# Two conditioning groups moved to the end of layer 0's experts, with squares summed a stage ahead

## The chip, the cores and the metric

One core of a Trainium2 chip runs the whole program. The metric is device time in microseconds (us). The kernel is one launch: one batch of 512 latent tokens with 256 context tokens and their conditioning vectors goes in, the latents after two blocks of two layers each come out, all in float32. The weights are read from HBM once.

## The reference, cut to what matters

Four layers follow each other. The first block's two layers are the ones that the change touches:

```python
for l in range(DEPTH):                        # DEPTH = 2, D = 1024
    mod_l = (silu_c @ w_ada[l] + b_ada[l])[:, None, :]      # w_ada [2, 1024, 6144]
    mod_c = (silu_cc @ w_ada[l] + b_ada[l])[None, None, :]
    sh1, sc1, g1, sh2, sc2, g2 = jnp.split(mod_l, 6, axis=-1)   # and the same of mod_c
    h_l = modulate(x_lat, norm_mix[l], sh1, sc1)            # rmsnorm(x, g) * (1 + sc) + sh
    h_c = modulate(x_ctx, norm_mix[l], sh1c, sc1c)
    # layer 0: mixer_ab (low-rank attention and grouped-query attention, rotary)
    # layer 1: mixer_na (attention to a window of neighbours and to the context)
    x_lat = x_lat + g1 * o_l
    h_l = modulate(x_lat, norm_ffn[l], sh2, sc2)
    if not last:                                            # layer 0: context too, 768 tokens
        x_ctx = x_ctx + g1c * o_c
        h_c = modulate(x_ctx, norm_ffn[l], sh2c, sc2c)
        y = hier_moe(tokens, w_rg[l], b_rg[l], w_re[l], b_re[l], w_gate[l], w_up[l], w_down[l])
        x_ctx, x_lat = x_ctx + g2c * y_c, x_lat + g2 * y_l
    else:                                                   # layer 1: the 512 latents
        x_lat = x_lat + g2 * hier_moe(h_l, ...)
return rmsnorm(x_lat, norm_final)

def hier_moe(h, ...):
    pg = softmax(h @ w_rg + b_rg); g_sel = argmax(pg)       # one of 4 groups
    le_sel = (h @ w_re + b_re)[group g_sel]                 # its 8 experts
    top_p, top_i = top_k(softmax(le_sel), 2)
    gate_w = p_gsel * top_p / sum(top_p)
    # each token goes to its two experts of 32:
    # y = sum gate_w * ((silu(x @ w_gate[e]) * (x @ w_up[e])) @ w_down[e])
```

A second block of two layers with other mixers (retention and sparse attention, an mLSTM) and dense feed-forward parts follows. The change does not touch it, apart from the first norm in it, which is the `norm_final` above.

## The kernel before, in words

**Layout.** Activations are feature-major: `P.x` (the residual) and `P.h` are tiles of 128 partitions x 8 chunks x 768 tokens, 256 of context first. The program is a sequence of stages, each a block with one program per engine, and they meet only in semaphores. `P.ahead` and `Ahead` objects hold the loads that a stage starts for the next one.

**Conditioning** (`class Conditioning`, lines 402 to 479). `w_ada` of both layers is 48 units of 1 MB, in six groups of eight (three groups a layer: shift and scale of the mixer; its gate and the shift of the experts; their scale and gate). `multiply` makes four matmuls of a unit (L448), which add up in one PSUM bank over the eight units of a group. `copy` (ScalarE, L455) takes the bank, `turn` (TensorE, L462) transposes it with four matmuls, `bias` (VectorE, L470 to L478) adds `b_ada` and makes the scales. A `Beside` object ties units and groups to the steps of a stage: after product n of the stage, PE multiplies the units listed for n, and the group listed for n is turned. Units 0 to 15 go with the first norm and the first projection, 16 and 17 with the norms of the low-rank parts, 18 to 36 with the low-rank up-projections (stage `ab_up`, `product_stage`, products at L1176), and 37 to 47 with the rotary stage (`rope_stage`), behind which the distance table's product stands (L2990).

**Norm** (`norm_stage`, line 555; `LatNorm`, line 679). Squares of eight chunks on ScalarE (L599, L604) and VectorE, their sums with matmuls against ones (L636, or L540 inside `QuadRows`), a root on ScalarE, a reciprocal on VectorE, a spread of the rows over the partitions on PE, then per chunk a scaling on VectorE and a shift on ScalarE (L617). `slab` gives POOL the split of the first weight slab of the next projection into two float32r parts (`FirstSlab.pool`, L243 and L245).

**Output stages** (`out_stage`, line 1686, on `split_stage`, line 877). Products of split float32r weights in eight PSUM banks (L996); VectorE takes each with `add_scaled` (L1227), which adds gate times product to `P.x`. ScalarE is free after the splits.

**Experts** (`expert_stage`, line 1843). The order of the work is laid down by `ExpertPlan`: 32 experts, two of them fixed first, the others in the order of their load, which is known only at run time. An expert is six pieces of 1 MB: gate and up in halves (4), down in halves (2). A ring of 18 slots holds them: 12 tiles of its own, three in `P.h`, two in `P.ahead`, one called `late`. SP issues the loads (L1800) in the plan's order; piece n behind the first 18 waits until the piece before it in its slot is freed (`used`). Twelve pieces and the route's inputs (L1830 to L1838) are issued in the norm stage. In order, the opening of the stage is:

1. PE: router logits of all tokens (L2221, 36 columns of weights against `P.h`), ScalarE and VectorE copy them, PE turns them (L2228). VectorE works out each token's experts, their counts, ranks (L2245, L2246) and slots.
2. PE turns `P.h` into rows of tokens (L2237), ScalarE copies them (L2347) and issues their store to a DRAM table (L2349).
3. PE finds the tokens of the two fixed experts with one-hot matmuls (L2252), VectorE makes their numbers, POOL gathers these rows from the DRAM table (L1879).
4. PE turns the gathered rows into features (`turn_rows`, L1936), makes the slot table for all experts (L2264), and starts the first visit.

A visit (`wide`, L1957, L1972, L1973; `down`, L1965, L1979, L1980) is 64 or fewer token slots of one expert; layer 0 has 41 of them, layer 1 has 36. ScalarE makes the silu (L1984), VectorE the product (L1987), ScalarE copies the result (L2387), POOL stores it to a table in DRAM (L2173, L2177) and gathers the rows of later visits. The first release of a ring slot comes with the first visit's first half.

The end of the stage is the mix: POOL gathers each token's two results (L2212), ScalarE scales one by its weight (L2421), VectorE adds the other (L2586), PE turns the tile back (L2338), VectorE adds it times the gate to `P.x` (L2598, eight instructions a tile). Layer 0 has six tiles of 128 tokens, layer 1 four.

On SP, the opening has these waits in the order of the pieces (L2121 to L2130):

```python
if n == plan.OWN - 1:  sp.wait_ge(turned_ready, NT)                  # P.h is free
if n == plan.OWN + 2:  [sp.wait_ge(rows_out[m], 16) for m in range(IN_AHEAD)]   # P.ahead is free
if n == plan.RING - 1: sp.wait_ge(first_slots, 1)                    # `late` is free
if n >= plan.RING:     sp.wait_ge(used, plan.freed[plan.after[n]])
```

**Order of the stages**, with the microseconds of the trace at which each runs: load and first norm 0 to 56, ab_in to 183, low-rank norms to 199, ab_up to 286, rotary to 319, attention to 541, ab_out 545 to 615, norm to 634, layer 0's experts to 1220, norm (`mod1`) to 1239, na_in to 1437, attention and na_out to 1609, norm to 1624, layer 1's experts to 2181, then the second block.

## Time and profile before

| | |
|---|---|
| median of 3 runs | 3599.15 us |
| lowest, highest | 3592.58, 3599.3 us |
| the profiled execution | 3606.98 us, span 3605.1 us |
| mean granted clock of TensorE | 0.928 |
| PE busy | 3134.4 us (87%) |
| PE's weight loads | 2150.2 us (60%) |
| VectorE, ScalarE, POOL busy | 1453.9 (40%), 761.6 (21%), 269.1 us (7%) |
| DMA | 675.08 MB, mean 187 GB/s |

Times of the rows below count from the start of the span. "Busy" of a matmul group is from its first start to its last end; PE is TensorE's matmuls, PEld its weight loads, which run beside them. PEclk is the granted clock as a share of the full 2.4 GHz, so 0.50 is 1.2 GHz. In the timelines each line is a group of like instructions on one engine: start, busy time, engine, line of the source, operation, out<-in, shape, count, and in brackets the idle time ahead of the group and what ended it. In the page's part of 40 slices a slice is 90 us.

### The profile page before, as it was taken

The page shows a single profiled execution, that of the slowest core. Times are in us where ns is not written, and L with a number is a line of the kernel's source. Part 1 is how long each engine was busy: PE and PEld are TensorE (multiplying, and loading weights), DVE is VectorE, ACT ScalarE, POOL GpSimd, SP SyncE. Part 2 cuts the span into 40 slices and gives each one's busy share as a digit, 9 for nine tenths or more (in the row PEclk, how much of TensorE's full clock was granted, in tenths as well). Part 3 has the DMA queues.
Part 4 walks back from the last instruction along what each step waited for, and adds up shares of the span by engine and source line. Part 5 has one row for each costly group of instructions (what it writes and reads, how often), then busy time and mean ns, then how long its engine had stood idle before and what let it go on. Part 6 is the DMA issues. An engine that isn't in the chain of part 4 may idle for free. (4 is left out here: it accounts for less than half of the span.)

```text
span 3605.1 us, 48930 instructions
## 1 busy us (share of the span) xinstructions
PE 3134.4 (87%) x19227; PEld 2150.2 (60%) x19227; DVE 1453.9 (40%) x2502; ACT 761.6 (21%) x1477; POOL 269.1 (7%) x471
## 2 busy tenths in 40 slices
PE   6999998798887599786987567988999999899998
PEld 5734677333333498663333336866888778678886
DVE  4225564300000533663000006455565574555555
ACT  3013571211111301631111111142110111221101
POOL 0000040111111200001111111000000000000000
PEclk8999999799998699897999878999999998999998
DMA  7176822999999424619999984212333175023321
GB/s 251 55 294 178 204 21 61 363 389 391 403 398 412 142 72 67 74 52 385 393 405 406 407 348 144 78 42 79 96 93 112 41 101 75 24 82 102 105 91 53
DMA packets 349969, 675.08 MB, mean 187 GB/s; under 512 B 68275, under 2 KB 275220, under 8 KB 294359
## 3 DMA queue, kind: packets, MB, share of 16 engines
q1 hardware_dynamic: 334396, 635.41, 52.8%
q0 software_dynamic: 13312, 31.49, 2.6%
q10 hardware_dynamic: 2067, 5.48, 0.4%
q8 instruction: 135, 2.21, 0.3%
q14 instruction: 59, 0.48, 0.0%
HBM read 639.00 MB, written 45.09 MB: 190 GB/s over the span
## 5 line engine op out<-in xcount | busy, mean ns | idle before, releaser
L3735 ACT ACTIVATE ffn_mixed<-ffn_mixed 128x512 f32<-128x512 f32 x44 | 27.8, 632 | 394.1 <-DVE ffn_mixed L3656 394.1
L1972 PE MATMUL moe0b_wide_ps<-moe_raw,moe0b_feats 128*64 128x512 f32 x208 | 98.2, 623 | 14.5 <-DMA moe_raw<-in_moe_w_up 14.5
L1987 DVE TENSOR_TENSOR moe0b_hidden<-moe0b_hidden,moe0b_wide_ps 64x512 f32<-64x512 f32 (+1 forms) x21 | 12.7, 603 | 239.1 <-ACT moe0b_hidden L1984 239.1
L1987 DVE TENSOR_TENSOR moe1b_hidden<-moe1b_hidden,moe1b_wide_ps 64x512 f32<-64x512 f32 (+1 forms) x18 | 10.3, 573 | 234.7 <-ACT moe1b_hidden L1984 234.7
L1987 DVE TENSOR_TENSOR moe0b_second<-moe0b_second,moe0b_wide_ps 64x512 f32<-64x512 f32 (+1 forms) x20 | 12.2, 611 | 227.6 <-ACT moe0b_second L1984 227.6
L1987 DVE TENSOR_TENSOR moe1b_second<-moe1b_second,moe1b_wide_ps 64x512 f32<-64x512 f32 (+1 forms) x18 | 10.3, 573 | 220.8 <-ACT moe1b_second L1984 220.8
L1973 PE MATMUL moe0b_wide_ps<-moe_raw,moe0b_feats 128*64 128x512 f32 x208 | 98.5, 624 | 0.0
L3653 DVE TENSOR_SCALAR ffn_mixed<-ffn_gate_ps,all_cols 128x512 f32<-128x512 f32 x44 | 35.6, 810 | 145.7 <-PE ffn_up_ps L3585 141.1
L1496 DVE TENSOR_REDUCE attn_top<-attn_scores 128x1 f32<-128x768 f32 (+1 forms) x96 | 72.4, 776 | 38.0 <-PE attn_scores L1409 38.0
L243 POOL CAST second_first_hi<-all_ahead 128x1024 fp32r<-128x1024 f32 x8 | 9.7, 1218 | 997.0 <-DMA all_ahead<-in_ffn_w_up 711.2
L1465 ACT ACTIVATE attn_probs_t<-attn_turned 128x512 f32<-128x512 f32 x112 | 63.4, 604 | 82.4 <-PE attn_turned L1423 82.4
L1972 PE MATMUL moe1b_wide_ps<-moe_raw,moe1b_second 128*64 128x512 f32 x120 | 63.0, 676 | 19.3 <-DMA moe_raw<-in_moe_w_up 19.2
L1979 PE MATMUL moe0b_result_ps<-moe_raw,moe0b_outputs 128*64 128x512 f32 x160 | 73.3, 598 | 4.2 <-DMA moe_raw<-in_moe_w_down 4.2
L1980 PE MATMUL moe0b_result_ps<-moe_raw,moe0b_outputs 128*64 128x512 f32 x160 | 73.4, 598 | 0.0
L1879 POOL DMA_INDIRECT moe_rows_in<-h_rows,moe_slot_token x73 | 69.7, 954 | 37.8 <-issue 21.7
L1456 ACT ACTIVATE l_cq<-attn_scores,attn_top 128x768 f32<-128x768 f32 (+1 forms) x96 | 71.7, 756 | 0.7 <-DVE attn_top L1496 0.7
L3656 DVE SCALAR_TENSOR_TENSOR ffn_mixed<-ffn_gate_ps,all_cols,ffn_mixed 128x511 f32<-128x511 f32 x88 | 65.9, 749 | 12.0 <-DVE ffn_mixed L3653 0.3
L1972 PEld LDWEIGHTS moe0b_wide_ps<-moe_raw,moe0b_feats 128*64 128x64 f32 x208 | 28.1, 143 | 71.2 <-issue 70.6
L3585 PE MATMUL ffn_gate_ps<-ffn_x_hi,ffn_w_hi 128*128 128x512 f32 x176 | 68.5, 389 | 0.0
L3585 PE MATMUL ffn_gate_ps<-ffn_x_lo,ffn_w_hi 128*128 128x512 f32 x176 | 68.5, 389 | 0.0
L3585 PE MATMUL ffn_gate_ps<-ffn_x_hi,ffn_w_lo 128*128 128x512 f32 x176 | 68.5, 389 | 0.0
L3585 PE MATMUL ffn_up_ps<-ffn_x_hi,ffn_w_hi 128*128 128x512 f32 x176 | 68.5, 389 | 0.0
(998 smaller groups left out, 8829.3 us busy)
## 6 DMA issues: line engine op xcount, KB each, us to landing
moe_raw<-in_moe_w_gate SPq DMA_DIRECT2D x88, 1024.0 KB, 28.5
moe_raw<-in_moe_w_up SPq DMA_DIRECT2D x88, 1024.0 KB, 28.9
moe_raw<-in_moe_w_down SPq DMA_DIRECT2D x86, 1024.0 KB, 29.1
all_ahead<-in_ffn_w_up SPq DMA_DIRECT2D x88, 512.0 KB, 5.1
all_h<-in_moe_w_gate SPq DMA_DIRECT2D x26, 1024.0 KB, 28.3
all_h<-in_w_ada SPq DMA_DIRECT2D x23, 1024.0 KB, 6.6
all_h<-in_moe_w_down SPq DMA_DIRECT2D x21, 1024.0 KB, 30.4
ffn_down<-in_ffn_w_down SPq DMA_DIRECT2D x40, 512.0 KB, 3.6
```

The lines of the kernel that those rows point to most:

```text
L1456: nc.scalar.activation(raised[k % LEAD][s][:, 0:t.keys], src[:, 0:t.keys], ACT.Exp, bias=column(top, k, s), scale=-1.0 if biased else 1.0, ...
L1465: nc.scalar.activation(probs_t[k % 2][:, at:end, :], turned[n % RING][:, 0:end - at, :], ACT.Copy).then_inc(turned_taken, 1)
L1496: V.tensor_reduce(column(top, k, s), scores[k % LEAD][s][:, 0:t.keys], AX.X, ALU.max, negate=True).then_inc(topped, 1)
L1879: nc.gpsimd.indirect_dma_start(rows, None, P.h_dram[0:n_tok, :], bass.IndirectOffsetOnAxis(ap=tokens, axis=0), bounds_check=n_tok - 1, oob ...
L1972: nc.tensor.matmul(wide_ps[n][LOW, :], x[:, c, :], gate[:, at], start=c == 0, stop=c == DC - 1)
L1973: last = nc.tensor.matmul(wide_ps[n][HIGH, :], x[:, c, :], up[:, at], start=c == 0, stop=c == DC - 1)
L1979: nc.tensor.matmul(result_ps[n][LOW, :], columns[n][:, c, :], rows[:, at:at + BANK], start=c == 0, stop=c == EC - 1)
L1980: last = nc.tensor.matmul(result_ps[n][HIGH, :], columns[n][:, c, :], rows[:, at + BANK:at + D], start=c == 0, stop=c == EC - 1)
L1987: return nc.vector.tensor_tensor(hidden[n][HIGH, 0:cols], hidden[n][HIGH, 0:cols], wide_ps[n][HIGH, 0:cols], ALU.mult)
L3585: last = nc.tensor.matmul(out[s][:], lhs_t, rhs, start=k == 0, stop=k == 3 * DC - 1)
L3653: V.tensor_scalar(mixed[s][:], gate_ps[s][:], col(taps + (FFN_CONV - 1) * FC), col(shift), ALU.mult, ALU.add).then_inc(conv_step, 1)
L3656: V.scalar_tensor_tensor(mixed[s][:, back:], gate_ps[s][:, 0:SEQ - back], col(taps + (FFN_CONV - 1 - back) * FC), mixed[s][:, back:], ALU. ...
```

## The change

It has five parts.

A. Units 32 to 47 of the conditioning, groups 4 and 5 (layer 1's mixer gate and all but the first shift and scale), move to the end of `expert_stage` of layer 0. Eleven are loaded into ring slots as the last visits free them, five behind the loop for experts with too many tokens. PE multiplies eight and turns group 4 ahead of the mix, and multiplies two behind each of the first four tiles' turns; group 5 is turned behind the last tile's turn. The copies and biases stand on ScalarE and VectorE ahead of the mix and at its end.

```diff
+LATE_GROUP = 4
-            ada.place("later", spare, range(2 * DC, ada.GROUPS * DC))
+            ada.place("later", spare, range(2 * DC, LATE_GROUP * DC))
...
                 product_stage(nc, P, "ab_up", loads, products, banks=5, ahead=tables,
-                              beside=Beside(ada, range(21, 42), {2 * n: (18 + n,) for n in range(19)}, {12: (2,), 28: (3,)}))
+                              beside=Beside(ada, range(21, 29), {5 * n: (18 + n,) for n in range(6)}, {28: (2,)}))
...
             rope_stage(nc, P, "rope", tables, items, spread,
-                       Beside(ada, range(42, 48), {n + 3: (37 + n,) for n in range(11)}, {6: (4,), 13: (5,)}), distances)
+                       Beside(ada, range(29, 32), {n + 3: (24 + n,) for n in range(8)}, {11: (3,)}), distances)
...
+                for u, n in zip(now, late_slots):                       # SP, behind the last expert piece
+                    sp.wait_ge(used, plan.freed[last_in[n]])
+                    ada.fetch(sp, u)
                 sp.wait_ge(used, 4 * N)
...
+                for u in then:                                          # SP, behind the extras
+                    ada.fetch(sp, u)
...
+                for u in late_units[0:DC]:                              # PE
+                    ada.multiply(pe, u)
+                if ada is not None:
+                    ada.turn(pe, LATE_GROUP)
                 for t in range(NT):
...
                     last.then_inc(mix_turned, 1)
+                    if t >= 2:
+                        tally_tile(t - 2)
+                    for u in late_units[DC + 2 * t:DC + 2 * t + 2]:
+                        ada.multiply(pe, u)
+                if len(late_units) > DC:
+                    ada.turn(pe, LATE_GROUP + 1)
+                tally_tile(NT - 2)
+                tally_tile(NT - 1)
...
+                if ada is not None:                                     # DVE
+                    ada.bias(dve, LATE_GROUP)
                 mix(0)
                 for t in range(NT):
                     if t + 1 < NT:
                         mix(t + 1)
+                    if t == NT - 1 and len(late_units) > DC:
+                        ada.bias(dve, LATE_GROUP + 1)
```

ScalarE has `ada.copy(act, LATE_GROUP)` ahead of its loop and `ada.copy(act, LATE_GROUP + 1)` behind it.

B. The two output stages ahead of the experts sum the squares of what they write and take the root. They have two, and one, PSUM banks fewer for it. The norm of the experts (`rooted=True`) then begins with the reciprocal.

```diff
+    def square(self, act, j):                                          # class Tally
+        out = self.squares[j % 2] if j else self.sums
+        self.nc.scalar.activation(out[:], self.P.x[:, j, self.all], ACT.Square).then_inc(self.squared, 1)
+    def add(self, dve, j):
+        if 0 < j < DC - 1:
+            self.nc.vector.tensor_tensor(self.sums[:], self.sums[:], self.squares[j % 2][:], ALU.add).then_inc(self.added, 1)
...
+        root, at = root_rows(self.P, self.n_tok), 0
+        for quads, total in zip(self.quads, self.total):
+            self.nc.scalar.activation(root[:, at:at + quads.m], total[:, 0:quads.m], ACT.Sqrt, scale=1.0 / D,
+                                      bias=self.P.eps[:, 0:1]).then_inc(self.rooted, 1)
```

The squares of seven chunks are added up before PE sums them against ones; the last chunk's are summed by themselves.

C. The router's logits are made in the norm stage from the rows that are not normalised yet. POOL multiplies the router's weights by the gains and by the shifts, PE multiplies with `P.x`, ScalarE copies, VectorE scales by the reciprocal root, and PE adds up the shifts' part.

```diff
+    def fold(self, pool):                                              # class EarlyLogits
+        pool.wait_ge(self.inputs.w_in, 2 * 16)
+        for w in self.which:
+            for out, by in ((self.gained, P.scale[:, self.l, 1, :, w]), (self.shifted, P.mod[:, self.l, 3 * DC:4 * DC, w])):
+                self.nc.gpsimd.tensor_tensor(out[:, w], w_route[:], by.unsqueeze(2).to_broadcast([PART, DC, self.W]), ALU.mult)
...
             for n in steps:                                             # norm_stage, PE
                 quads[n].spread(by_half[n], P.pick, root[:, cols[n]], root_spread)
+            if logits is not None:
+                for c in range(C):
+                    logits.multiply(pe, c, jobs)
+                logits.shift(pe)
```

D. The first visits' features are made with one-hot matmuls from the rows in SBUF, 48 of them in layer 0 and 32 in layer 1, instead of the gather. The slot table stands behind the first visit's wide half. The rows are stored with the columns in another order, so that `turn_rows` reads them contiguously.

```diff
+                def first_rows():
+                    pe.wait_ge(rows_act, NT)
+                    pe.wait_ge(first_made, 1)
+                    for c in range(DC):
+                        for t in range(NT):
+                            by_chunk = row_places[t].rearrange("t (c p) -> t c p", c=DC)
+                            hot = first_hot[:, t * FIXED:(t + 1) * FIXED, :].rearrange("p e n -> p (e n)")
+                            last = nc.tensor.matmul(feats_ps[:, c, :], by_chunk[:, c, :], hot, start=t == 0, stop=t == NT - 1)
+                    last.then_inc(feats_ready, 1)
...
-                pe.wait_ge(rows_act, NT)
-                rows(0)
-                slot_table()
+                first_rows()
                 for s in range(N):
+                    if s == 1:
+                        slot_table()
...
                     if n == plan.OWN + 2:                               # SP
+                        sp.wait_ge(feats_ready, 1)
                         for m in range(IN_AHEAD):
                             sp.wait_ge(rows_out[m], 16)
                     if n == plan.RING - 1:
-                        sp.wait_ge(first_slots, 1)
```

E. Both mixes square the finished tiles (ScalarE), sum them (PE, `tally_tile`, eight matmuls a tile) and take one root at the end. The norm `mod1` and the final norm begin with the reciprocal (`rooted=True`, `made=True`).

```diff
+                def square_tile(t):                                     # ScalarE
+                    act.wait_ge(mix_added, (t + 1) * DC)
+                    nc.scalar.activation(squares[t % 2], P.x[:, :, at:at + PART], ACT.Square).then_inc(mix_squared, 1)
...
+                act.wait_ge(mix_summed, NT)
+                nc.scalar.activation(root_rows(P, n_tok), result_ps[0][:, 0:n_root], ACT.Sqrt, scale=1.0 / D, bias=P.eps[:, 0:1])
```

## Rows read from the trace of the kernel before

**Rows 1.** Page, busy share of the DMA engines in 40 slices of 90 us

```profile
DMA  7176822999999424619999984212333175023321
```

**Rows 2.** DMA view of 700 to 1100

```profile
DMA packets 24908, 158.17 MB, mean 395 GB/s; under 512 B 4331, under 2 KB 4339, under 8 KB 6891
...
moe_rows_in<-h_rows,moe_slot_token POOLq DMA_INDIRECT x34, 8.4
```

**Rows 3.** Windows: stretch, length, PE, PEld, DVE, ACT, POOL, PEclk, DMA, GB/s

```profile
200.00:240.00 40.00, 40.00 (x164) 16.25 (x162) 5.17 (x9) 3.52 (x9) 0.00 (x0) 1.00 0.74 270
...
674.00:680.00 6.00, 6.00 (x30) 5.93 (x28) 0.22 (x2) 2.31 (x2) 1.71 (x4) 0.50 0.71 294
...
1200.00:1210.00 10.00, 5.91 (x26) 5.12 (x27) 8.08 (x21) 3.44 (x3) 4.15 (x5) 0.50 0.77 262
```

**Rows 4.** Timeline of ab_up and the end of the rotary stage

```profile
226.26 1.07 PE L448 MATMUL ada_acc<-all_h,all_cond 128*32 128x512 f32 x8
...
227.25 4.11 PE L1176 MATMUL ab_up_bank<-l_cq,ab_up_wq 128*96 128x512 f32 x12
...
232.32 0.65 PE L462 MATMUL ada_turned<-all_ident,ada_rows 128*128 128x128 f32 x4
...
316.80 1.24 PE L2990 MATMUL rope_distance_acc<-ab_up_wkv,rope_bias 33*8 33x512 f32 x4
```

**Rows 5.** Timeline, end of ab_out and opening of layer 0's experts

```profile
614.33 0.75 DVE L1227 SCALAR_TENSOR_TENSOR all_x<-ab_out_bank,all_mod,all_x 128x512 f32<-128x512 f32 x1 [4.98 <-PE ab_out_bank L996]
...
622.20 0.43 SPq L1800 DMA_DIRECT2D moe_raw<-in_moe_w_gate  x1
...
634.51 7.70 PE L2221 MATMUL moe0b_feats_ps<-all_h,moe_w_route 128*36 128x384 f32 x32 [9.59 <-PEq L558]
...
655.33 1.02 ACT L2347 ACTIVATE moe_rows_in<-moe0b_wide_ps 128x1024 f32<-128x1024 f32 x1 [0.68 <-PE moe0b_wide_ps L2237]
...
674.90 5.22 PE L2264 MATMUL moe0b_slot_ps<-moe0b_outputs,moe0b_second 128*128 128x64 f32 x24
```

**Rows 6.** GB/s in 40 slices, 625 to 705 and 1640 to 1706

```profile
GB/s 430 418 434 422 430 422 418 418 410 422 426 403 418 428 430 408 416 418 270 365 422 416 422 436 414 426 242 0 0 154 211 276 328 270 406 422 418 426 422 414
...
GB/s 412 427 427 432 422 427 429 415 442 422 427 425 417 412 427 422 253 25 104 161 181 415 370 283 355 437 407 422 412 432 417 412 437 412 358 315 278 387 402 447
```

**Rows 7.** Timeline of PE, the first visit of layer 0 and of layer 1

```profile
680.05 1.12 PE L1972 MATMUL moe0b_wide_ps<-moe_raw,moe0b_feats 128*64 128x512 f32 x1
...
1667.40 1.12 PE L1972 MATMUL moe1b_wide_ps<-moe_raw,moe1b_feats 128*64 128x512 f32 x1
```

**Rows 8.** Timeline, end of mod1, and start of the second block

```profile
1233.64 5.33 ACT L617 ACTIVATE all_h<-mod_squares,all_mod 128x512 f32<-128x512 f32 x8
...
1234.79 2.36 POOL L245 TENSOR_TENSOR na_v_first_lo<-all_ahead,na_v_first_hi 128x1024 fp32r<-128x1024 f32 x1
...
2193.59 0.79 PE L954 MATMUL even_in_bank<-even_in_x_hi,second_first_hi 128*128 128x512 f32 x1 [5.86 <-POOL second_first_lo L245]
```

**Rows 9.** Timeline of PE in 1636 to 1640, ranks of layer 1

```profile
1637.30 0.49 PE L2245 MATMUL moe1b_result_ps<-moe1b_second,moe_earlier 128*128 128x128 f32 x2 [1.36 <-DVE moe1b_second L2461]
...
1637.63 0.39 PE L2246 MATMUL moe1b_result_ps<-moe1b_second,all_ones 128*128 128x128 f32 x2
```

**Rows 10.** Timeline of VectorE, mix of layer 0

```profile
1196.67 1.28 DVE L2586 SCALAR_TENSOR_TENSOR moe_raw<-moe_raw,moe_weight 128x1024 f32<-128x1024 f32 x1 [21.18 <-ACT moe_raw L2421]
...
1218.26 2.16 DVE L2598 SCALAR_TENSOR_TENSOR all_x<-moe0b_wide_ps,all_mod,all_x 128x128 f32<-128x128 f32 x8
```

**Rows 11.** DMA of 1150 to 1190 in 40 slices, and of 1184 to 1221

```profile
GB/s 426 410 410 410 414 434 401 426 434 401 434 410 422 438 426 393 401 393 369 377 360 377 344 336 303 287 238 139 123 82 49 41 39 39 16 0 8 66 0 0
...
DMA packets 1779, 6.39 MB, mean 173 GB/s; under 512 B 224, under 2 KB 224, under 8 KB 1776
```

**Rows 12.** DMA view of 634 to 700, first gathers

```profile
moe_rows_in<-h_rows,moe_slot_token POOLq DMA_INDIRECT x4, 3.8
```

**Rows 13.** Timeline of PE, the norm of the second block's feed-forward

```profile
2483.18 1.95 PE L540 MATMUL ffn_norm_single<-all_x,all_ones 128*32 128x128 f32 x64 [1.05 <-PEq L883]
```

306 lines of the change are left out of this document (219 added, 87 removed).

## Prediction, made before the changed kernel ran

> **What bounds the kernel now.** On one core no single engine bounds all 3605.1 us, so I went stage by stage. The page's slices come first [rows 1]: DMA stands at 9 in slices 7 to 12 and 18 to 23, the experts of layers 0 and 1, at about 400 GB/s, and low elsewhere. There the stream of expert weights is the clock: 700 to 1100 moved 158.17 MB at a mean of 395 GB/s [rows 2]. In the low-rank projections it is the reverse: 200 to 240 has PE busy 40.00 of 40 at clock 1.00, DMA at 0.74 [rows 3]. So a unit of conditioning costs PE time where it sits today, and DMA time where it is moved to. The chain of waits ends in the store and says nothing about either place.
>
> **Projections and rotary stage.** A unit's four matmuls start at 226.26 and the next product at 227.25, so one unit holds PE for 0.99 us; a group's turn is busy for 0.65 us, of which I count 0.5, since neighbours overlap [rows 4]. ab_up keeps 6 of 19 units and one of two turns: 13 x 0.99 + 0.5 = 13.4 us less. The rotary stage keeps 8 of 11 units, and VectorE paces it. What goes is its end: the distance product waits until 316.80 for the last unit, its copy and its turn [rows 4], about 2.4 us after the last item's product. With 0.1 us for each of three steps I take 2.7 us. Together **-16.1** (bounds -14 and -17). Loads left out here save nothing: DMA had room.
>
> **Squares and root in the output stages.** ScalarE and VectorE are idle between the takes of the out stage, so seven of the eight squares, the adds and their matmuls are free; DVE reaches the slab split at most 1.7 us later, which PE's queue covers. Behind the last take (614.33 + 0.75 [rows 5]) stand one square of 768 columns (about 0.9), eight small matmuls and two roots: 2.4 us in layer 0, 2.0 in layer 1. The weight stream starts later by that, since its first load is issued 6.9 us into the next stage (622.20 [rows 5]).
>
> **Opening of the experts.** The stream's idle time here is the prize. From 677 to 692 it had little to do (242, 0, 0, 154, 211, 276, 328, 270 GB/s in 2 us slices), against about 422; with the dip near 662 the lost part is 10.0 us [rows 6]. In layer 1 the same sum is 6.4 us [rows 6]. The ring of 18 slots was full and the first release came only with the first visit, which starts at 680.05 in layer 0 and at 1667.40 in layer 1 [rows 7].
> The new chain for layer 0, on the old time axis: the stage begins at 617.8; reciprocal and spread are done near 621.4. Route weights land about 621.5, and POOL folds them in four products of 288 columns. A POOL product of 1024 columns takes 2.36 us [rows 8], so 0.7 each at least; I take 0.9, bound 1.5. Then come the logits' 7.70 us [rows 5], four copies (1.5) and sixteen matmuls for the offset (3.5 to 7). The turned logits stand at about 638, 4 to 5 us early, and the last row copy ends near 652 instead of 656.35. Now 48 matmuls of 128 columns make the first features. With 128 columns one took 0.33 us from start to start in layer 1, just after PE had run at the fast level [rows 9]; the slot table's twelve take 5.22 us, 0.435 each, for 64 columns at clock 0.50 [rows 5, 3]. So 0.33 fast and at most 0.66 slow: 15.8 to 31.7 us. PE is busy with turns before that, so I take 5 us of the slow level and 40 at the fast: 18.2 us. Features at 670.2, first visit at 671.3, 8.7 us early.
> Fifteen pieces and the row writes keep DMA busy until about 671.7 (start 2.4 late), and the last three ring slots, which now wait for the features, are asked for at 670.2. So the hole closes: -10.0, -1.2 for the gather that goes (0.52 MB), +2.4: **-8.8**. Layer 1 has 32 such matmuls, 13 us, features near 1652: -6.4 - 1.2 + 2.0 = **-5.6**. The slot table moves behind the first visit; eight freed pieces cover it.
> The twelve matmuls of the slot table ran with PE 6.00 and PEld 5.93 of 6 us busy [rows 3], the loads hidden behind the products. The Trainium skill (TensorE: Matmul & The Clock Gate, Part 3: Packing small matmuls) says that a weight load overlaps a running matmul only in another row group. By that each of the 48 would pay its load too, and the features would come later by some 12 us, as in rival 2; this trace disagrees.
>
> **End of layer 0's experts.** Before: the last expert piece lands about 1182 (the stream's fading end, below), DVE's first mix starts at 1196.67, its last add ends at 1220.42 [rows 10]. Now 16 units, 16.8 MB, are queued behind the last pieces. In 1184 to 1221 DMA moved only 6.39 MB, and from 1168 to 1182 the stream had faded from 369 to 82 GB/s [rows 11]; I read that as some engines ending early, and about 3.2 MB fit into it. So 16.8 - 3.2 + 6.8 (gathers, last store) = 20.4 MB at 420 GB/s = 48.5 us behind 1184, 1232.5 for the mean engine and 1238 for the slowest, if the same 5 to 6 us of lag stay. The first eight units gate everything: bias of group 4 stands ahead of the first mix on DVE, its copy ahead of the first scaling on ACT, its multiplies ahead of the first turn on PE. They land about 1208, as the gathers share the engines from 1192 on; a gather took 8.4 us under the stream and 3.8 in a window with the hole in it [rows 2, 12]. The first mix comes at about 1211 instead of 1196.67.
> The Trainium skill (DMA: Bandwidth & Descriptors, Queues, rings and completion order) says that each DMA engine alternates, a packet at a time, between the queues that have work. By it every gather waits behind units for as long as those last; the trace agrees with its 8.4 us, and rival 3 is its worst case.
> Units 46 and 47 stand ahead of tile 4's turn. Behind 1238 come a unit (1.0), two turns (1.1 fast, 1.96 slow), tallies, the second group's turn and bias, the last add (2.16), square (1.15), tally and root. A tally of a 128-token tile is eight dependent matmuls: the like of a chain of 64 records in 1.95 us [rows 13], at most twice that at the slow level. PE ran at 0.50 in 1200 to 1210 [rows 3]. Fast the stage ends at 1252, slow at 1261; I take 1253.4, **+33** (bounds +20, if every byte fits and PE is fast, and +41).
> After it, the norm saves 6 us of its own, but POOL's split of the first slab ends at 1237.15, 16.4 us into a stage whose last shift ends at 1238.97, 18.3 us into it [rows 8]: **-1.9**.
>
> **End of layer 1's experts.** Tallies follow turns on PE: the last turn is 2.6 us late, three tallies at 2 to 3.9, square, root. **+6.9** (bounds +4, +13). The final norm's squares go, but PE's start at 2193.59 waits for POOL's slab [rows 8]: **-0.4**.
>
> **Sum.** -16.1 - 8.8 + 33 - 1.9 - 5.6 + 6.9 - 0.4 = **+7.1 us**. The profiled execution took 3606.98 us (span 3605.1), 7.8 over the median of 3599.15, so it would read 3614; against the median I give 3606. Differences under 0.2%, 7.2 us, can't be told from none.
>
> **Rivals.**
> 1. *The late units hide* (0.22; the other side). Their bytes fill the fading stream and the gathers' gaps, the last lands at 1232 and PE runs fast behind it: end at 1240.4, +20 instead of +33, sum -6; with the opening's lower bounds -9. It decides if unit 47 lands before about 1231. For it: 6.39 MB in 37 us is 173 GB/s, 41% of 420 [rows 11]. Against: the bytes must still pass one after another, and the first mix waits for eight units.
> 2. *PE stays at 1.2 GHz* (0.15). The first features take 27 us or more, the hole in layer 0 stays (+9 to +13), and the tails take 8 and 6 us more: sum +30 to +34, or +16 where only the opening is slow. For it: 0.50 in 674 to 680 and in 1200 to 1210 [rows 3].
> 3. *Gathers starve* (0.08). The units' larger packets hold the gathers back, so the last tiles follow all units: +10 on the tail, sum +17.
> 4. *The experts run at PE's pace* (0.05): the first visits come 8.7 and 13 us early and all of that is gained in place of 8.8 and 5.6, sum 0 and below. Against it: DMA at 9 through both stages [rows 1].
>
> **Numbers.** The forecast keeps 0.50 with its own range 3597 to 3614; half of it is beyond 0.2%. Slower: 0.25 + 0.15 + 0.08 and a little = 0.49. Same: 0.25 + 0.09 = 0.34. Faster: 0.17, from rivals 1 and 4 at their better bounds. The range reaches to rival 1's lower end and into rival 2: 3590 to 3623.
>
> **What would show it.** ab_up and the rotary stage 16 us shorter; first visit near 671 less the 16 us, and no DMA slice below 200 GB/s in the hole's place; DVE's first mix of layer 0 at about 29 us behind the last expert piece instead of 14.5; DMA at 9 up to the last unit; a stage end 33 us later counted from the last expert piece. The forecast is wrong if the first mix comes within 5 us of its old distance, if the hole in the opening stays, or if ab_up does not shrink.

## The result, and the profile after the change

The changed kernel has a median of 3609.73 us in 14 runs, the kernel before 3596.64 us in 14 runs beside them. The medians are 13.1 us apart; the ratio of the runs is 1.0034 with a 95% interval of 1.0027 to 1.0041, and by it the change costs 12.2 us (9.7 to 14.7). The forecast was 3606.0 with a range of 3590 to 3623, the right side (slower by over 0.2% had the chance 0.49), and +7.1 us where +12.2 came.

The two profiled executions lie closer, 3605.1 and 3607.9 us of span. The profiled execution of before stands 10.3 us above the median of its kernel's runs (3606.98 against 3596.64), the one after at its median (3609.77 against 3609.73). Part of that gap has a place, found below in the attention stage.

The page after, spans and slices:

```profile
span 3607.9 us, 49100 instructions
PE 3150.8 (87%) x19287; PEld 2166.6 (60%) x19287; DVE 1456.6 (40%) x2499; ACT 772.5 (21%) x1482; POOL 270.1 (7%) x475
DMA  7145823999999524619999984212333174023321
```

Slices 3 and 4, the projections, have less to load than in [rows 1], and the stretch at 9 begins a little sooner. The steps between marks that both traces have, in us. The last result copy is ScalarE's copy of the last visit's result; the root is the square root that part E puts behind the mix:

| from, to | before | after | difference | forecast |
|---|---|---|---|---|
| start to ab_up | 199.64 | 199.02 | -0.6 | 0 |
| ab_up and rotary, to the first scores | 119.27 | 102.13 | -17.1 | -16.1 |
| attention, to ab_out's first product | 226.77 | 221.49 | -5.3 | 0 |
| ab_out, opening, visits of layer 0, to the last result copy | 639.27 | 633.63 | -5.6 | -8.8 |
| to the last add, and after the change to the root | 35.47 | 66.67 | +31.2 | +33 |
| mod1, to na_in's first product | 20.82 | 17.70 | -3.1 | -1.9 |
| layer 1 up to na_out's last add | 368.07 | 366.27 | -1.8 | 0 |
| opening and visits of layer 1, to the last result copy | 544.23 | 544.85 | +0.6 | -5.6 |
| to even_in's first split product | 40.05 | 43.13 | +3.1 | +6.5 |
| the rest | 1411.5 | 1413.0 | +1.5 | 0 |

**Projections.** TensorE's timeline after the change, at the end of the rotary stage:

```profile
295.04 0.60 PE L463 MATMUL ada_turned<-all_ident,ada_rows 128*128 128x128 f32 x4
...
296.72 1.13 PE L1386 MATMUL rope_turned<-l_gk,rope_swap_b 128*128 128x512 f32 x2 [0.21 <-DVE l_gq L1403]
297.77 1.24 PE L3208 MATMUL rope_distance_acc<-ab_up_wkv,rope_bias 33*8 33x512 f32 x4
```

The distance product now stands right behind the last item's product, and no unit is between them as in [rows 4]. 316.80 became 297.77.

**Openings.** GB/s in 2 us slices of 625 to 705 after the change, and of 1640 to 1706 in 1.65 us:

```profile
GB/s 436 424 408 438 412 428 428 422 424 438 414 426 418 434 418 434 379 272 266 268 277 281 414 397 414 418 420 322 293 266 365 416 428 426 418 426 410 410 406 289
```

```profile
GB/s 412 425 417 432 427 427 427 432 412 422 432 417 417 422 278 281 278 261 293 266 276 340 422 422 407 402 340 310 305 422 417 416 416 417 412 412 432 427 412 420
```

The zeros of [rows 6] are gone, and no slice is under 200. In their place is a plateau of 261 to 293 for some 10 to 12 us. The first visits start far earlier than in [rows 7]:

```profile
642.22 0.64 PE L2136 MATMUL moe0b_wide_ps<-moe_raw,moe0b_feats 128*64 128x512 f32 x1 [1.18 <-ACT moe0b_feats L2564]
```

That is 50.2 us behind ab_out's last add (592.02), where it was 65.0; in layer 1 it is 41.4 instead of 58.1. Of these 14.8 and 16.7 us the last result copies keep 5.6 and none.

**End of layer 0's experts.** The timeline of the changed kernel, from the last result copy to the second mix:

```profile
1155.89 0.38 ACT L2585 ACTIVATE moe0b_outputs<-moe0b_result_ps 128x256 f32<-128x256 f32 x1 [4.92 <-PE moe0b_result_ps L2129]
...
1164.41 0.99 POOL L2393 DMA_INDIRECT moe_raw<-y_rows,moe_row_of  x1 [6.36 <-DMA y_rows<-moe0b_outputs,moe_quarter_rows]
...
1166.71 1.28 ACT L2623 ACT_TABLE_LOAD   x1 [10.44 <-issue]
...
1172.45 3.64 PE L449 MATMUL moe_route<-all_h,all_cond 128*32 128x512 f32 x16 [16.63 <-issue]
...
1179.45 2.76 PE L449 MATMUL moe_route<-moe_raw,all_cond 128*32 128x512 f32 x24
...
1182.35 0.60 ACT L456 ACTIVATE moe_raw<-moe_route 128x512 f32<-128x512 f32 x1 [14.14 <-PE moe_route L449]
...
1183.70 0.19 DVE L471 TENSOR_TENSOR all_mod<-moe_columns_ps,all_cols 128x32 f32<-128x32 f32 x1 [36.96 <-PE moe_columns_ps L463]
1184.02 1.28 DVE L2800 SCALAR_TENSOR_TENSOR moe_raw<-moe_raw,moe_weight 128x1024 f32<-128x1024 f32 x1
```

The first mix starts 27.75 us behind the last copy (1156.27), against 11.72 before [rows 10]. But the eight units before it wait for no load: TensorE stood 16.63 us with no releaser ("issue"), and then multiplied them back to back. What it did in these 16.63 us is the loop for experts with too many tokens, 23 passes that are all empty here, 0.72 us each; ScalarE needs 10.44 us for them, 0.45 each. Behind the first mix the tiles came every 7 to 9 us where it had been 3 to 5, each waiting for its gathers:

```profile
moe_raw<-y_rows,moe_row_of POOLq DMA_INDIRECT x8, 13.8
```

Before, the same DMA view of 1185 to 1221 has 5.3 us to landing. Two things could thus set the end, TensorE's chain or the bytes; e5 to e7 below are for that.

### The profile page after: what moved, and what is told of

It reads as the page before. It is cut to its first block and busy times, and to the rows that moved or that the text cites. A ratio compares the mean times of both kernels' runs of the same rounds, so it can differ in the third digit from the quotient of the medians.

```text
span 3607.9 us, 49100 instructions
## 1 busy us (share of the span) xinstructions
PE 3150.8 (87%) x19287; PEld 2166.6 (60%) x19287; DVE 1456.6 (40%) x2499; ACT 772.5 (21%) x1482; POOL 270.1 (7%) x475
## 5 line engine op out<-in xcount | busy, mean ns | idle before, releaser
L2151 DVE TENSOR_TENSOR moe1b_second<-moe1b_second,moe1b_wide_ps 64x512 f32<-64x512 f32 (+1 forms) x18 | 10.3, 573 | 239.9 <-ACT moe1b_second L2148 239.9
L2151 DVE TENSOR_TENSOR moe0b_hidden<-moe0b_hidden,moe0b_wide_ps 64x512 f32<-64x512 f32 (+1 forms) x21 | 12.7, 602 | 233.2 <-ACT moe0b_hidden L2148 233.2
L2151 DVE TENSOR_TENSOR moe0b_second<-moe0b_second,moe0b_wide_ps 64x512 f32<-64x512 f32 (+1 forms) x20 | 12.2, 611 | 232.8 <-ACT moe0b_second L2148 232.8
L2151 DVE TENSOR_TENSOR moe1b_hidden<-moe1b_hidden,moe1b_wide_ps 64x512 f32<-64x512 f32 (+1 forms) x18 | 10.3, 573 | 224.0 <-ACT moe1b_hidden L2148 223.9
L3803 PE MATMUL ffn_gate_ps<-ffn_x_hi,ffn_w_hi 128*128 128x512 f32 x176 | 68.5, 389 | 0.0
L3803 PE MATMUL ffn_gate_ps<-ffn_x_lo,ffn_w_hi 128*128 128x512 f32 x176 | 68.5, 389 | 0.0
L3803 PE MATMUL ffn_gate_ps<-ffn_x_hi,ffn_w_lo 128*128 128x512 f32 x176 | 68.5, 389 | 0.0
L3803 PE MATMUL ffn_up_ps<-ffn_x_hi,ffn_w_hi 128*128 128x512 f32 x176 | 68.5, 389 | 0.0
```

The lines of the kernel that those rows point to most:

```text
L2151: return nc.vector.tensor_tensor(hidden[n][HIGH, 0:cols], hidden[n][HIGH, 0:cols], wide_ps[n][HIGH, 0:cols], ALU.mult)
L3803: last = nc.tensor.matmul(out[s][:], lhs_t, rhs, start=k == 0, stop=k == 3 * DC - 1)
```

## The experiments

### One part at a time

**e1_units_back.** The changed kernel without A.

```diff
-LATE_GROUP = 4
+LATE_GROUP = 6
-   beside=Beside(ada, range(21, 29), {5 * n: (18 + n,) for n in range(6)}, {28: (2,)})
+   beside=Beside(ada, range(21, 42), {2 * n: (18 + n,) for n in range(19)}, {12: (2,), 28: (3,)})
-   Beside(ada, range(29, 32), {n + 3: (24 + n,) for n in range(8)}, {11: (3,)})
+   Beside(ada, range(42, 48), {n + 3: (37 + n,) for n in range(11)}, {6: (4,), 13: (5,)})
-   expert_stage(nc, A, K, P, 0, 0, both, ada)
+   expert_stage(nc, A, K, P, 0, 0, both)
```

> The changed kernel with part A undone: the sixteen units are back in ab_up and the rotary stage, and parts B to E stay. Theory (A is the whole loss): in the profiles A saves 17.8 us ahead of the attention and costs about 27.5 us of the 31.2 us by which the end of layer 0's experts grew, so about 10 of the 12 us of the ratio are A's. Then this kernel is at +2 us against the kernel before (0 to +4), and the end of layer 0's experts, from the last result copy to the root, takes about 39 us instead of 66.7. Rival 1 (B to D cost time, as the first visits' one-hot matmuls and the late start of the stream give back more than they save): +6 us or more. Rival 2 (the tallies lengthen the tail by more than the 3 us seen in layer 1): the tail of layer 0 stays above 45 us.

Measured: 3600.15 us, ratio 1.0007 (0.9993 to 1.0021), +2.5 us. From the last copy to the root it took 42.1 us (38.6 to the last add). With A gone, 9.7 of the 12.2 us are gone by the two ratios. The interval here, -2.5 to +7.6 us, doesn't put rival 1 of this text (B to D cost 6 us or more) out by itself; that of e3 below, which ends at +2.9, does. The tail was 3 us longer than expected: ScalarE was 14.03 us in the empty passes here.

**e2_units_only.** The kernel before with A alone (the diff of A under "The change", on the old banks).

> The kernel before with part A alone: sixteen units at the end of layer 0's experts, all else as before. Theory (A is the whole loss, and the parts add up): +10 us (+8 to +13), the tail of layer 0 from the last result copy to the last add at about 63 us instead of 35.5. Rival (A hides when nothing else stands in the tail, as in the first rival of the prediction: the loss is the tallies' and turns' together): +3 us or less, a tail under 55 us.

Measured: 3605.1 us, ratio 1.0015 (1.0003 to 1.0027), +5.4 us (+1 to +10). The tail was 62.5 us to the last add, as the theory said, so A does not hide even when it is alone there. The time fell short of +8, though the steps of the profile (ab_up and rotary 102.11, tail +27.0) make +9.9 without the attention stage, and +3.0 with it (219.91, 6.9 less). So A costs 5.4 us alone and 9.7 by the difference of e1; the two intervals overlap.

**e3_openings_only.** e1_units_back without E: no `tally_tile`, `square_tile` and root in the mix, `rooted=True` taken from mod1 and `made=True` from the final norm.

> Parts B, C and D alone: squares in the output stages, early logits, first rows from SBUF; the units are back and the mixes make no squares, so that the norm behind layer 0's experts and the final norm make their own. Theory: layer 0's opening gives 5.6 us (stage start to last result copy), layer 1's opening nothing (+0.6), so -5 us (-2 to -7) against the kernel before, and about 5 us under e1_units_back if the root behind the mix costs as much as in layer 1's end (+3.1) with nothing won back. Rival (the squares of part E pay for themselves at mod1, -3.1 and +3.5): the same as e1_units_back within 1.5 us.

Measured: 3599.33 us, ratio 0.9995 (0.9981 to 1.0008), -1.8 us. That is just short of the -2 to -7 expected; the interval, -6.8 to +2.9, holds both that and nothing. From ab_out's first product to the last copy it took 635.23, 4.0 us less than before, and then the first mix came 15.2 us behind it instead of 11.7, again with 14.03 us of ScalarE in the passes. E costs 4.3 us by the ratios of e1 and this run, but their intervals overlap, so that is not shown. In the traces in layer 0 the root adds 3.5 and mod1 gives 3.1 back (20.82 to 17.70), while in layer 1 the last add to even_in's product takes 13.9 us here and 15.8 with E.

**e4_eight_units.** The changed kernel with `LATE_GROUP = 5`: units 40 to 47 late, two behind each of the first four turns, nothing ahead of the first mix.

> The changed kernel with only group 5, eight units, late, multiplied two behind each of the first four turns; group 4 stays in ab_up and the rotary stage, so nothing stands ahead of the first mix. Theory (the bytes set the price: the tail moves what it has at about 400 GB/s): 8.4 MB fewer give back 20 to 21 of the 27.5 us, while ab_up and the rotary stage lose about half of their 17.8 us: against the kernel with all units back -1 to -2 us, so about 0 against the kernel before and 11 us under the changed kernel. Rival (the price is one of waits and turns, so much a unit): half of the tail's 27.5 us stays, +5 us against the kernel with all units back.

Measured: 3599.97 us, ratio 1.0001 (0.9988 to 1.0015), +0.4 us. The tail is 50.3 us to the root, the gathers land in 6.4 us (median), and ab_up with the rotary stage takes 111.95. The whole time is the theory's. The tail is between the two: by the theory it gives back 20 to 21 us of the changed kernel's 66.7, to about 46, by the rival half of 27.5, to about 53, and it gave back 16.4. Against e1_units_back (42.1) half the units cost 8.1 us in the tail where sixteen cost 24.5, which looks like a price for what does not fit into the stage's own gaps. But the 42.1 hold 3.6 us more of empty passes than the other two (14.03 against 10.44 on ScalarE); from 38.5 the prices are 11.8 and 28.2, or 1.5 and 1.8 us a unit. So this run does not separate a price by bytes from a price by unit.

### What sets the end: bytes or TensorE

**e5_no_late_loads.** The changed kernel without the loads; the multiplies work on what lies in the slots.

```diff
-                for u, n in zip(now, late_slots):
-                    sp.wait_ge(used, plan.freed[last_in[n]])
-                    ada.fetch(sp, u)
...
-                for u in then:
-                    ada.fetch(sp, u)
...
-        pe.wait_ge(self.into[u], self.arrival[u])
+        if g < LATE_GROUP:
+            pe.wait_ge(self.into[u], self.arrival[u])
```

> The changed kernel without the loads of the sixteen late units: the multiplies, turns, copies and biases stay where they are and work on what lies in the slots, so the conditioning of groups 4 and 5 is not computed. Measured in the profile from the last result copy of layer 0 (1156.27 in the changed kernel) to the end of the root (1222.94), 66.7 us, of which 27.8 go by up to the first mix. Theory T1 (bytes set the price): without 16.8 MB the tail is 36 to 44 us, and the first mix comes 15 to 17 us behind the last copy. Theory T2 (TensorE sets it: it walks 16.6 us through the empty passes of the loop for experts with too many tokens, then multiplies eight units for 9.8 us, then turns and biases): the first mix stays at 26 to 28 us, and only the tiles behind it come at 4 us each instead of 7: a tail of 52 to 56 us.

Measured, in layer 0 only (layer 1 runs with other conditioning, and its router's choices change the whole time, 3682 us): the first mix came 26.8 us behind the last copy and the root ended at 54.7, both in T2's bounds. The timeline of ScalarE and VectorE in this run:

```profile
1180.70 0.60 ACT L457 ACTIVATE moe_raw<-moe_route 128x512 f32<-128x512 f32 x1 [13.20 <-PE moe_route L450]
...
1182.37 1.28 DVE L2796 SCALAR_TENSOR_TENSOR moe_raw<-moe_raw,moe_weight 128x1024 f32<-128x1024 f32 x1
```

T2 is right for the first mix: it is late with no byte loaded. The tail is 12 us shorter than the 66.7 with the loads, so from there on it is not TensorE alone.

**e6_narrow_products.** The changed kernel with all loads; of each late group seven of the eight units are multiplied over 32 columns instead of 512.

```diff
+        cols = BANK if g < LATE_GROUP or c == 0 else 32
...
-            self.nc.tensor.matmul(self.acc[g % 2][q * QUAD:(q + 1) * QUAD, :], self.P.cond[:, c, :],
-                                  self.slot[u][:, q * BANK:(q + 1) * BANK], ...)
+            self.nc.tensor.matmul(self.acc[g % 2][q * QUAD:(q + 1) * QUAD, 0:cols], self.P.cond[:, c, :],
+                                  self.slot[u][:, q * BANK:q * BANK + cols], ...)
```

> The changed kernel with all loads, but of each late group only the first unit is multiplied over 512 columns, the other seven over 32, so the conditioning of groups 4 and 5 is not computed. It takes some 14 us of TensorE's time out of the tail and leaves every load, wait and turn. T1 (bytes): units 38 and 39 land when they did, so the first mix is at 25 to 27 us behind the last copy and the tail at 63 to 67 us. T2 (TensorE): the first mix at 19 to 21 us and the tail at 56 to 60 us.

Measured: the first mix at 23.2 us, 4.5 earlier, and the root at 68.5 us, not earlier at all; 3611.24 us in its one run. The first mix lies between the two theories (25 to 27, 19 to 21). The end is T1's, 1.5 us above its bound.

**e7_loop_guarded.** One test ahead of the loop, on all five engines:

```diff
-                with pe.Fori(0, EXTRA) as i:
-                    with pe.If(extras > i):
+                with pe.If(extras > 0):
+                    with pe.Fori(0, EXTRA) as i:
+                        with pe.If(extras > i):
```

> The changed kernel with each engine's loop for experts with too many tokens (23 passes in layer 0, 15 in layer 1, all empty with these inputs) put behind one test that any such expert exists, so that an engine walks past it at once. In the profile of the changed kernel ScalarE takes 10.44 us for the 23 passes and 6.72 for the 15, 0.45 a pass, TensorE 16.6 for the 23. T1 (bytes): TensorE starts the late units up to 16 us sooner, but the eighth lands at about 1180 as before, and the sum of bytes is the same: the tail 1 to 4 us shorter, the whole kernel -1 to -5 us against the changed kernel, so +8 to +11 us against the kernel before. T2 (TensorE's loop gates the tail): 10 to 14 us shorter, so about even with the kernel before.

Measured: 3610.97 us, ratio 1.0043 (1.0027 to 1.0059). The timeline of TensorE behind the last product of the experts, and in the last line VectorE's first mix:

```profile
1155.06 1.94 PE L449 MATMUL moe_route<-all_h,all_cond 128*32 128x512 f32 x8 [0.87 <-DMA all_h<-in_w_ada]
...
1171.87 1.93 PE L449 MATMUL moe_route<-moe_raw,all_cond 128*32 128x512 f32 x8 [1.83 <-DMA moe_raw<-in_w_ada]
1175.64 1.93 PE L449 MATMUL moe_route<-moe_raw,all_cond 128*32 128x512 f32 x8 [1.84 <-DMA moe_raw<-in_w_ada]
...
1179.63 1.28 DVE L2805 SCALAR_TENSOR_TENSOR moe_raw<-moe_raw,moe_weight 128x1024 f32<-128x1024 f32 x1
```

The 16.6 us are gone, and TensorE now waits for each unit: the eighth is multiplied at 1175.64, 21 us behind the last copy (1154.64). The first mix is at 25.0, the root at 66.65 behind the copy, against 66.67 without the test. So TensorE's chain and the stream of units end within 3 us of each other at the first mix, and from there the stream with its gathers (14.1 us to landing) sets the end. The last of the sixteen loads shows it best. The changed kernel issues it 23.5 us behind the last copy, at 1179.8; here, with SyncE's passes gone too, it is issued 12.7 us behind, at 1167.4. The DMA view of either, with the us from issue to landing:

```profile
moe_late<-in_w_ada SPq DMA_DIRECT2D x1, 1024.0 KB, 27.4
```

```profile
moe_late<-in_w_ada SPq DMA_DIRECT2D x1, 1024.0 KB, 38.4
```

It lands 50.9 and 51.1 us behind the copy, so 10.8 us of head start are worth nothing. In both the last gather lands at 53.8, and the root ends 12.9 us behind that. The forecast of no gain from TensorE's time was T1's, and the size of it, 1 to 4 us, was still too much.

### The empty passes, and the best of the parts

**e8_units_back_guarded.** e1_units_back with that test.

> e1_units_back with the same test ahead of the loops. There the first mix of layer 0 started 16.6 us behind the last result copy, and the trace shows ScalarE 14.03 us without a releaser and then a table load of 1.3 us, while the gathers of the first tile were issued 4 us behind the copy and need 6.6 us in the kernel before. If the empty passes on ScalarE and TensorE are what holds the mix (theory), the first mix comes at 11 to 12 us behind the copy and the tail is 5 to 7 us shorter in layer 0 and at most 1 in layer 1: -5 to -7 us against e1_units_back, about -4 us against the kernel before. Rival (the time is the gathers', and the passes only fill it): within 1 us of e1_units_back.

Its timeline against that of e1_units_back, ScalarE in both:

```profile
1172.41 0.38 ACT L2588 ACTIVATE moe0b_outputs<-moe0b_result_ps 128x256 f32<-128x256 f32 x1 [4.92 <-PE moe0b_result_ps L2129]
1173.36 1.28 ACT L2627 ACT_TABLE_LOAD   x1 [0.57 <-issue]
```

```profile
1177.69 0.38 ACT L2585 ACTIVATE moe0b_outputs<-moe0b_result_ps 128x256 f32<-128x256 f32 x1 [4.91 <-PE moe0b_result_ps L2129]
...
1192.11 1.28 ACT L2623 ACT_TABLE_LOAD   x1 [14.03 <-issue]
```

14.03 us became 0.57, the first mix came 11.9 us behind the copy instead of 16.6, and the tail to the root was 37.4 instead of 42.1: in the trace the mechanism is as expected. In the times it is not: 3597.75 us, ratio 1.0007 (0.9998 to 1.0017), the same as without the test. The expected -4 us against the kernel before is outside that interval. Where the 4.7 us of the trace go in the times is open.

**e9_openings_guarded.** e3_openings_only with the test, in search of a version that beats both.

> Parts B, C and D, the units back in ab_up and the rotary stage, no squares in the mixes, and the one test ahead of the empty passes. Theory: layer 0's opening gives 5 us by the last result copy (a lead of 1.6 MB of the stream), layer 1's nothing; without part E the end of layer 1 up to the second block's first product is back at 40 us from the last copy, instead of 44; without the passes the first mix of layer 0 is 12 us behind the copy and TensorE's first turn is no longer 3 us late. In all -7 us against the kernel before (-4 to -9), the fastest version so far. Rival (what one part gives is taken back at a place that I have not seen, as with part E in layer 1): even with the kernel before within 2 us.

Measured: 3591.78 us beside 3593.61 of the kernel before, ratio 1.0001 (0.9989 to 1.0013). A miss: no gain that can be told, though its profiled span is 3589.1 us against 3605.1 and 3599.8 of the kernel before. No version here beats the kernel before by more than its measurement can tell.

**e10_before_again.** The kernel before, unchanged, for a second profile.

> The kernel before as it is, for a second profile of its attention stage. In the profiles of the kernel before, of e1_units_back and of e3_openings_only TensorE stands still for about 3.5 us in that stage with no releaser shown and then runs some 5 us at a granted clock of 0.50, and the stage takes 226.8 us; in six others, among them e8_units_back_guarded with the same work in and ahead of this stage, it takes 219 to 224. If the stop belongs to the place of TensorE's program in memory or to the number of its instructions, it is here again at the same product and the stage takes 226 to 227 us. If it comes and goes from one execution to the next, the stage takes 219 to 224 us here, or stops elsewhere.

The timeline of TensorE in its attention stage, and the two windows around:

```profile
373.80 0.93 PE L1433 MATMUL attn_mixed<-attn_probs_t,l_va 128*64 128x128 f32 x13
378.36 0.37 PE L1433 MATMUL attn_mixed<-attn_probs_t,l_va 128*64 128x128 f32 x1 [3.63 <-issue]
```

```profile
359.00:379.00 20.00, 16.26 (x117) 11.48 (x117) 11.46 (x21) 10.64 (x24) 0.00 (x0) 0.96 0.48 51
379.00:399.00 20.00, 18.91 (x123) 13.94 (x123) 9.88 (x24) 9.58 (x24) 0.00 (x0) 0.87 0.72 178
```

The stop is there again, at the same product, and the stage takes 226.93 us (226.77 in the first profile). In these two executions, then, it comes with the program. It goes when units leave ab_up (after, e2, e4, e5, e6, e7: 218.7 to 224.1), but it goes too in e8 and e9 (220.0), whose program up to this stage is that of e1 and e3 (226.9 and 226.7): only later code differs. The windows of the first profile of before show what it costs:

```profile
372.00:376.00 4.00, 4.00 (x31) 2.97 (x31) 2.17 (x3) 1.78 (x5) 0.00 (x0) 1.00 0.47 49
376.00:380.00 4.00, 0.88 (x17) 0.64 (x12) 1.57 (x4) 1.93 (x5) 0.00 (x0) 0.98 0.48 54
380.00:384.00 4.00, 3.65 (x12) 2.89 (x12) 0.85 (x2) 0.39 (x1) 0.00 (x0) 0.50 0.48 54
384.00:388.00 4.00, 4.00 (x34) 3.45 (x33) 0.94 (x4) 2.09 (x7) 0.00 (x0) 0.66 0.22 29
```

3.5 us without work, then some 5 us at a granted clock of 0.50. The timeline names nothing that TensorE waits for in the 3.5 us, but the DMA view has a queue that it calls "instruction". In all four traces with the stop (the two of the kernel before, e1 and e3) a packet of 16 KB of this queue starts 1.2 to 1.5 us into the stop and takes 0.9 us, and TensorE's next product follows 1.4 to 1.5 us behind its end. In these four, and in e8 and e9 with the same program up to there, the packet before it starts 38.7 to 39.0 us behind the first scores. The packet itself starts 59.1 to 59.4 us behind them in the four; in e8 and e9 it starts at 44.7, and TensorE doesn't stop. The view of 377 to 380 of before, and of 362 to 365 of e8:

```profile
q8 instruction: 1, 0.02, 1.8%
```

```profile
q8 instruction: 1, 0.02, 1.9%
```

So the stop looks like a wait for instructions that come late. That the packet is TensorE's, and why it comes 14.5 us later in one program than in the other, no run shows.

Nor is it shown how many of the other timed runs have the stop, since the trace of one execution a kernel is kept. Those with the stop stand 10.3 (before), 8.0 (e10, against 3593.61), 8.3 (e1) and 1.7 us (e3) above the median of their kernel's runs, the six without it (changed, e2, e4, e7, e8, e9) between -0.8 and +3.2. And e8's profiled span is 8.9 us under e1's where the ratios are the same. Both would fit if most of the other runs don't have it, and e3 fits less well.

The second profile also tells how far one pair of profiles carries. From ab_out's first product to the last result copy of layer 0 the kernel before took 639.27 us in the first and 636.39 in the second. The three profiles with the old opening (these and e2) took 636.4 to 640.1, the nine with the new one 631.3 to 635.2: on the mean 4.8 us less. In layer 1 the step from na_out's last add took 543.5 to 544.3 with the old opening and 543.0 to 544.9 with the new one.

## Why the prediction was right, and where its steps failed

**ab_up and rotary stage: right.** -17.1 against -16.1, just past the outer bound of -17. The part of the last unit, copy and turn before the distance product was as read.

**Attention: not in the sum.** -5.3 in the profiles, by the stop above. The step that failed is an assumption left unsaid, that a stage whose code isn't touched takes the same time.

**Opening of layer 0: the mechanism right, the size off.** "Features at 670.2, first visit at 671.3, 8.7 us early" erred on the safe side. The 48 matmuls took 12.5 us, not 18.2:

```profile
628.55 2.04 PE L2432 MATMUL moe0b_feats_ps<-moe_late,all_ahead 128*128 128x128 f32 x8 [3.29 <-DVE moe_late L2699]
...
640.66 0.39 PE L2432 MATMUL moe0b_feats_ps<-moe_late,moe_rows_in 128*128 128x128 f32 x2
```

```profile
628.00:642.00 14.00, 12.50 (x96) 12.34 (x96) 12.70 (x41) 0.85 (x1) 0.00 (x0) 0.88 1.02 424
```

That is 0.26 us each from start to start; the 0.33 that I took was that of two matmuls of [rows 9], a pair too short to tell. PEld is busy 12.34 us beside PE's 12.50, so the weight loads are hidden here too. The rule of the Trainium skill (TensorE: Matmul & The Clock Gate, Part 3: Packing small matmuls), that a weight load overlaps a running matmul only in another row group, does not hold in this trace either; the same part also names a background weight buffer for loads that go ahead, and the trace fits that.

The term that failed is "So the hole closes: -10.0". The hole was not empty. In 676 to 692 of before, and in 656 to 672 after, the DMA view shows in turn

```profile
q1 hardware_dynamic: 305, 2.20, 41.6%
q0 software_dynamic: 280, 0.82, 19.5%
```

```profile
q1 hardware_dynamic: 591, 4.31, 83.4%
q0 software_dynamic: 288, 0.83, 19.0%
```

The same 0.82 to 0.83 MB of gathers for the second to fifth visits ran inside the hole before and run beside the stream now, as the plateau near 275 GB/s. At 422 the plateau's 11 us lack 3.8 us of stream, and this the forecast had counted as won. Summed over windows of 10 us from ab_out's last add, the changed kernel is 0.95 MB behind at 40 us (the root, 2.3 us of stream), 1.66 MB ahead at 70 us, and 0.9 to 2.1 MB ahead to the end of the stage, mostly 1.5 to 2.0: some 4 us, with 1.2 for the gather that is gone about the 5.6 seen. Against the second profile of the kernel before (e10) the same sum is 0.9 MB behind, 1.2 ahead and then 0.3 to 0.9 ahead, and the step 2.8 us shorter instead of 5.6. That the opening gives less than the forecast 8.8 holds by both; by how much it does not.

**Opening of layer 1: wrong.** -5.6 was forecast, +0.6 came. The same sum from na_out's last add has it 1.2 MB behind at 30 to 50 us, 2.9 us of stream where 2.0 was assumed for the root, and 0.1 to 1.2 MB behind at 80 us and later. Against e10 the two are 0.85 MB, the 2.0 us as assumed, and even to 0.9 behind. The term that failed here too is the hole, "-6.4": if the gathers take as much of it as in layer 0, 2.6 us are left (an estimate, 6.4 - 3.8), and the late start took them. The first visit's 16.7 us are worth nothing against a stream that doesn't end sooner; rival 4, in which they would be gained whole, is out in both layers.

**End of layer 0's experts: +31.2 against +33, but by other steps.** The forecast had the first mix at 1211, 26 us behind the last copy (1184.95), because eight units would land so late; it was 27.75, and e5 shows the same 26.8 with no load at all. The step that failed is "The first eight units gate everything", by the time at which they land: TensorE's empty passes (16.6 us) and eight products (9.8 us, at a mean granted clock of 0.72) do. That walk through the passes stands in TensorE's timeline of the kernel before too, ahead of its first turn, 3 us behind the mix that it could have started with, and the forecast has no term for it:

```profile
1201.06 1.96 PE L2338 MATMUL moe0b_feats_ps<-all_ident,moe_raw 128*128 128x128 f32 x8 [16.56 <-issue]
```

With the passes gone (e7) the loads gate it 2.8 us earlier, and it makes no difference to the end. That the end is the bytes' was right: e6 and e7 take TensorE's time out and end at 68.5 and 66.7, and gathers take 13.8 us to land beside the units. The forecast had the slowest engine done at 1238, 53 us behind the last copy; the last gather lands at 53.8. (In [rows 11] the 82 GB/s belong to 1179, at 1182 it is 39; the 3.2 MB are right.) So the size of this term came near by the right mechanism, and the gate of its first mix by luck. The Trainium skill (DMA: Bandwidth & Descriptors, Queues, rings and completion order) has each engine alternate between queues with work; the landing times of 5.3 us alone and 13.8 us beside units agree in kind. Rival 3, "gathers starve", was half in the sum already: its mechanism is here, its extra 10 us are not.

Rival 1, the late units hide, is out by e2 and by the root at 66.7. Rival 2, TensorE at 1.2 GHz, is out: the granted clock is 0.87 in 614.5 to 642, and 0.81 in 1184 to 1220, where it was 0.50 before. There TensorE is busy for 27.6 us instead of 11.5 (in 1185 to 1221), with units to multiply between the turns.

**mod1 and layer 1's end.** -3.1 against -1.9, and +3.1 against +6.5: both of the predicted sign. The tallies of layer 1 were faster than their bounds; the last add came at 27.35 us behind the last copy as before (27.36).

**The sum.** The misses in the openings (+9.4) and in layer 1's end (-3.4), the attention (-5.3) and the small ones leave the profiles at +2.8. The ratio says +12.2. That the forecast lies only 5 us from it is in part luck: the openings missed by more, and other misses went the other way. The 5.3 of the attention, if the timed runs don't have it, makes 8.1 of it, and 4 us stay open: the medians of the kernel before moved from 3593.6 to 3598.1 between sessions, and parts of 5 us are at the edge of what these runs can tell. By the ratios of the parts, A alone is +5.4, B to D -1.8 and E +4.3, together 7.9 with some 5 us of doubt on each.

## What to carry to other kernels

Before moving a transfer's time into a hole of the stream, look at what else uses the hole: bytes ahead of the old kernel at equal distance from a mark tell the gain, the start of the first visit doesn't. And take a second profile of the old kernel before a difference of 5 us in one stage is believed: here it moved by 2.9. Loads that are moved to the end of a stream-bound stage are paid there by their bytes (the last of sixteen lands 51 us behind the last copy, whether it is issued early or late), and they slow the small gathers that the end waits for. Behind the last visit look at the engines' "issue" time too: an empty loop of 23 passes is 10 to 17 us on an engine.

## What was not expected of the hardware

- An empty pass of a loop with a test costs 0.45 us on ScalarE (10.44 us for 23, 6.72 for 15) and 0.72 on TensorE (16.63 for 23); in two kernels ScalarE took 14.03 us for the same 23, which no run explains.
- TensorE can stop for 3.5 us in the middle of a stage with no wait in the timeline, at the same product in two profiles of one program, and lose it in a program that differs only in later code. In the four traces that have it, a 16 KB packet of the DMA view's "instruction" queue lands 1.4 to 1.5 us before TensorE goes on. With the clock's fall behind it that is 5 to 7 us.
- 48 accumulating matmuls of 128 columns, each with another weight, ran in 12.5 us, 0.26 us each, with their weight loads hidden.
